# A mixture-of-experts block: single-pass products for the slot table, two gathers moved into the router's stage, the output bias moved behind the first turned rows

## What is computed

```python
logits = xt @ w_router + b_router                      # 512 tokens, 32 experts
top_v, top_e = lax.top_k(logits, 4)
weights = jax.nn.softmax(top_v, axis=-1)
# each expert e, on the rows of its tokens:
hcat = x_pad[tok] @ w1[e] + b1[e]                      # 1024 -> 2048
act = x_glu * sigmoid(1.702 * x_glu) * (x_lin + 1.0)
y = act @ w2[e] + b2[e]                                # 1024 -> 1024
out = sum over the 4 chosen experts of y * weight
x = x + g_f * out
```

## Time and profile before

| | us |
|---|---|
| median of 3 runs | 3260.22 |
| lowest and highest of them | 3252.39, 3261.88 |
| the profiled execution | 3259.38 |
| its span | 3257.5 |
| TensorE busy in the span | 3024.5 (93%) |
| VectorE busy | 2098.2 (64%) |
| ScalarE busy | 1633.2 (50%) |
| GpSimd busy | 229.2 (7%) |
| DMA, mean over the span | 187 GB/s |

### The profile page before, as it was taken

One profiled execution on the slowest core, in us unless ns is written; L12 is line 12 of the kernel. 1 busy time (PEld: TensorE's weight loads), 2 busy tenths in 40 slices (PEclk: granted clock), 3 DMA queues, 4 the chain that ended last, 5 costly groups with the idle time before them and its releaser, 6 DMA issues. The chain is left out here.

```text
span 3257.5 us, 46689 instructions
## 1 busy us (share of the span) xinstructions
PE 3024.5 (93%) x18822; PEld 2410.6 (74%) x18822; DVE 2098.2 (64%) x2112; ACT 1633.2 (50%) x1797; POOL 229.2 (7%) x141
## 2 busy tenths in 40 slices
PE   7999999879999999999999829788999999989999
PEld 2677788658877888778878717687778887778877
DVE  6536643558899999999999845466363345356633
ACT  7445532337777777777777624222453343333321
POOL 0000000001111111111111000342000000000000
PEclk9899999869999999999999969898998898999999
DMA  8321122249999999999999752000221112323322
GB/s 359 112 64 59 53 91 91 106 194 355 382 371 365 372 378 378 370 369 373 380 367 376 285 196 65 15 4 3 88 64 56 59 54 78 104 77 102 93 78 77
DMA packets 212528, 607.97 MB, mean 187 GB/s; under 512 B 9522, under 2 KB 117042, under 8 KB 176020
## 3 DMA queue, kind: packets, MB, share of 16 engines
q1 hardware_dynamic: 203008, 571.66, 47.9%
q0 software_dynamic: 9216, 33.56, 2.7%
q10 hardware_dynamic: 148, 0.53, 0.0%
HBM read 582.62 MB, written 23.10 MB: 186 GB/s over the span
## 5 line engine op out<-in xcount | busy, mean ns | idle before, releaser
L2436 DVE TENSOR_TENSOR weight_ring_part<-weight_ring,weight_ring_part 128x2048 fp32r<-128x2048 f32 x380 | 851.4, 2289 | 106.1 <-ACT weight_ring_part L2374 106.1
L2374 ACT ACTIVATE weight_ring_part<-weight_ring 128x2048 fp32r<-128x2048 f32 x380 | 711.9, 1914 | 254.6 <-DMA weight_ring<-in_w 134.0
L193 PE MATMUL ps<-weight_ring_part 128*128 128x512 f32 x1456 | 583.2, 401 | 0.0
L293 DVE TENSOR_TENSOR weight_ring_part<-weight_ring,weight_ring_part 128x2048 fp32r<-128x2048 f32 x135 | 307.5, 2283 | 292.4 <-ACT weight_ring_part L290 290.0
L189 PE MATMUL ps<-weight_ring_part,gathered_hi 128*128 128x512 f32 x1024 | 403.9, 394 | 0.0
L192 PE MATMUL ps<-weight_ring_part,gathered_lo 128*128 128x512 f32 x1024 | 400.3, 391 | 0.0
L193 PE MATMUL ps<-weight_ring_part,gathered_hi 128*128 128x512 f32 x1024 | 400.1, 391 | 0.0
L189 PE MATMUL ps<-h1T_hi,weight_ring_part 128*128 128x512 f32 x872 | 361.4, 414 | 3.2 <-DVE weight_ring_part L293 1.7
L192 PE MATMUL ps<-h1T_hi,weight_ring_part 128*128 128x512 f32 x872 | 351.5, 403 | 0.0
L290 ACT ACTIVATE weight_ring_part<-weight_ring 128x2048 fp32r<-128x2048 f32 x135 | 256.6, 1903 | 160.8 <-PE ps L193 108.3
L193 PEld LDWEIGHTS ps<-weight_ring_part 128*128 128x128 f32 x1456 | 279.3, 192 | 68.9
(11 more groups left out here) (474 smaller groups left out, 4412.5 us busy)
## 6 DMA issues: line engine op xcount, KB each, us to landing
weight_ring<-in_w SPq DMA_DIRECT2D x190, 2048.0 KB, 9.7
weight_ring<-in_w_in SPq DMA_DIRECT2D x58, 1024.0 KB, 5.3
weight_ring<-in_w_ada SPq DMA_DIRECT2D x24, 1024.0 KB, 15.0
weight_ring<-in_w_ffn_up SPq DMA_DIRECT2D x44, 512.0 KB, 4.7
weight_ring<-in_w_ffn_down SPq DMA_DIRECT2D x11, 1024.0 KB, 4.9
weight_ring<-in_w_branch SPq DMA_DIRECT2D x6, 1024.0 KB, 5.1
x_tok<-in_x SPq DMA_DIRECT2D x2, 2048.0 KB, 14.0
weight_ring<-in_w_out SPq DMA_DIRECT2D x4, 1024.0 KB, 5.2
```

Source lines behind the costliest of these rows:

```text
L193: return nc.tensor.matmul(out, x[0], y[1], start=False, stop=stop)
L293: self.nc.vector.tensor_tensor(lo, full, hi, ALU.subtract).then_inc(self.split, 1)
L2374: nc.scalar.activation(hi_half(h), full_half(h), ACT.Copy).then_inc(w_rounded, 1)
L2436: nc.vector.tensor_tensor(lo_half(h), full_half(h), hi_half(h), ALU.subtract).then_inc(w_split, 1)
```

## The change

Three edits.

1. `slot_hot` and `hot_row` become rounded fp32 tiles, so that each product of the slot table is one pass. Its numbers have to be small whole numbers for that: the choice is coded as j + 1 instead of j - 2048, and `read_tables` puts the rest back with a prepared column `spare_row`. A new drain behind the reading of `x_at` gives GpSimd leave.
2. `x_rows` and the semaphores `gathered` are made ahead of the router's stage, and GpSimd issues the gathers of experts 0 and 1 in it, as soon as `x_at` is read and the rows are stored. In the experts' stage it begins with the gather of expert 2.
3. All four bias products use banks 6 and 7 and each waits for the addition of the one before. The first stands behind `turn_inputs(0)`; the second behind the first up product; the third behind `turn_inputs` of expert 1; the fourth behind the turned hidden rows of the first turn. VectorE adds the first behind the split of the first rows, the second where the last was, the third between the hidden rows and the split of the second rows, the fourth at the end of the first turn.

```diff
-        hot_row = sb(moe, "hot_row", [P, TOPK, TT, 2, E])
+        hot_row = sb(moe, "hot_row", [P, TOPK, TT, 2, E], F32R)
+        x_rows = sb(moe, "gathered_rows", [P, 2, D])
+        gathered = [ctx.enter_context(nc.semaphore(f"gathered{n}")) for n in range(2)]
...
-        spare = sb(moe, "spare_row", [P, E])
+        spare = sb(moe, "spare", [P, E])
+        spare_row = sb(moe, "spare_row", [P, 1])
...
-        slot_hot = sb(moe, "slot_hot", [P, TOPK * TT, P])
+        slot_hot = sb(moe, "slot_hot", [P, TOPK * TT, P], F32R)
...
-        def read_tables(nc, dve):
+        def read_tables(nc, dve, read):
 
             nc.vector.tensor_copy(x_at[:, :], ps[:, 5, 0:E])
-            nc.vector.tensor_scalar(spare[:, :], ps[:, 5, E:2 * E], 0.0, col("token"), ALU.is_ge, ALU.mult)
+            dve.drain().then_inc(read, 1)
+            nc.vector.tensor_scalar(spare[:, :], ps[:, 5, E:2 * E], 0.0, spare_row[:, :], ALU.is_equal, ALU.mult)
             dve.drain()
-            nc.vector.scalar_tensor_tensor(spare[:, :], ps[:, 5, E:2 * E], float(TOPK * T), spare[:, :], ALU.add, ALU.add)
+            nc.vector.scalar_tensor_tensor(spare[:, :], ps[:, 5, E:2 * E], -1.0, spare[:, :], ALU.add, ALU.add)
...
+            @block.gpsimd
+            def _(pool):
+                pool.wait_ge(x_at_ready, 1)
+                pool.wait_ge(h_stored, 16 * TT)
+                for e in range(2):
+                    nc.gpsimd.indirect_dma_start(x_rows[:, e, :], None, h_rows, bass.IndirectOffsetOnAxis(x_at[:, e:e + 1], 0))\
+                        .then_inc(gathered[e], 16)
...
-                    nc.scalar.activation(hot_row[:, j, :, 1, :], hot[:, j], ACT.Copy, scale=float(j - TOPK * T)).then_inc(rows_made, 1)
+                    nc.scalar.activation(hot_row[:, j, :, 1, :], hot[:, j], ACT.Copy, scale=float(j + 1)).then_inc(rows_made, 1)
...
+                nc.vector.tensor_scalar(spare_row[:, :], col("token"), float(TOPK * T + 1), None, ALU.add)
...
-                read_tables(nc, dve)
+                read_tables(nc, dve, x_at_ready)
...
-                b2_banks = lambda t: ps[:, (0, 2, 6, 6)[t]:(0, 2, 6, 6)[t] + 2, :]
+                b2_banks = ps[:, 6:8, :]
...
-                        for e in range(3):
+                        for e in range(0 if rounds else 2, 3):
                             gather(r, e)
...
                     def output_bias(t_):
-                        if t_ == 3:
-                            pe.wait_ge(b2_added, 3)
+                        if t_:
+                            pe.wait_ge(b2_added, t_)
...
-                        else:
-                            output_bias(0)
-                            output_bias(1)
                         if rounds:
                             pe.wait_ge(table_read, t.block)
                         turn_inputs(0, t.nth)
                         if not rounds:
-                            output_bias(2)
+                            output_bias(0)
 
                     def turn(t):
                         if not t.last:
                             up(t)
                         if t.first and not rounds:
-                            output_bias(3)
+                            output_bias(1)
                         if not t.first:
                             pe.wait_ge(hid_ready, t.i * 2)
                         if t.more:
                             turn_inputs(1 - t.parity, t.nth_after)
+                            if t.first and not rounds:
+                                output_bias(2)
...
                                 last.then_inc(turned, 1)
+                            if t.first and not rounds:
+                                output_bias(3)
...
                         if not rounds:
-                            add_bias(0)
-                            add_bias(1)
-                            dve.drain().then_inc(up_read, 1)
+                            nc.vector.engine_nop().then_inc(up_read, 1)
...
                         split_inputs(t.i + 1)
                         if not rounds:
-                            add_bias(2)
+                            add_bias(0)
...
                             if t.first and not rounds:
-                                add_bias(3)
+                                add_bias(1)
                             split_half(t, 11)
...
                                     .then_inc(hidden_ready, 1)
+                            if t.first and not rounds:
+                                add_bias(2)
                             if t.more:
                                 split_inputs(t.i + 2)
                             if not t.first:
                                 for o in range(12, 16):
                                     split_half(t, o)
+                            if t.first and not rounds:
+                                add_bias(3)
```

More of the change, by code:

```diff
@@ L1936, in build @@
                    "logits_ready", "hot_made", "rows_made", "tops_ready", "exps_ready", "chosen_ready", "places_ready", "slots_ready", "table_ready",
-                   "weights_ready", "weights_turned") as (
+                   "weights_ready", "weights_turned", "x_at_ready") as (
                 block, *norm_sems, tables_loaded, first_rounded, hf_even, hf_odd, h_turned, h_ready, h_stored, turned_logits, logits_copied,
                 logits_ready, hot_made, rows_made, tops_ready, exps_ready, chosen_ready, places_ready, slots_ready, table_ready,
-                weights_ready, weights_turned):
+                weights_ready, weights_turned, x_at_ready):
             norm_turned = norm_sems[3]
@@ L2109, in build @@
         experts = ctx.enter_context(ExitStack())
-        x_rows = sb(experts, "gathered_rows", [P, 2, D])
         xg_hi = sb(experts, "gathered_hi", [P, DK, P], F32R)
@@ L2121, in build @@
         LIMIT = 7.0
-        gathered = [ctx.enter_context(nc.semaphore(f"gathered{n}")) for n in range(2)]
         y_stored = [ctx.enter_context(nc.semaphore(f"y_stored{n}")) for n in range(2)]
@@ L2194, in experts_pass @@
                        "glu_ready", "act_ready", "hidden_ready", "turned", "hid_rounded", "hid_ready", "y_read", "y_free",
-                       "b1_loaded", "b1_rounded", "b1_ready", "w_rounded", "w_split", "b2_summed", "b2_added") as (
+                       "b1_loaded", "b1_rounded", "b1_ready", "w_rounded", "w_split", "b2_summed", "b2_added", "x_at_ready") as (
                     block, hot_ready, table_ready, table_read, x_turned, xg_rounded, xg_ready, up_read,
                     glu_ready, act_ready, hidden_ready, turned, hid_rounded, hid_ready, y_read, y_free,
-                    b1_loaded, b1_rounded, b1_ready, w_rounded, w_split, b2_summed, b2_added):
-                b2_banks = lambda t: ps[:, (0, 2, 6, 6)[t]:(0, 2, 6, 6)[t] + 2, :]
+                    b1_loaded, b1_rounded, b1_ready, w_rounded, w_split, b2_summed, b2_added, x_at_ready):
+                b2_banks = ps[:, 6:8, :]
                 b1 = a["b1"][0]
@@ L2319, in output_bias @@
                     def output_bias(t_):
-                        if t_ == 3:
-                            pe.wait_ge(b2_added, 3)
+                        if t_:
+                            pe.wait_ge(b2_added, t_)
                         for j in range(2):
-                            last = nc.tensor.matmul(b2_banks(t_)[:, j, :], weight_et[:, P * t_:P * t_ + P],
+                            last = nc.tensor.matmul(b2_banks[:, j, :], weight_et[:, P * t_:P * t_ + P],
                                                     bias_rows2[:, 512 * j:512 * j + 512], start=True, stop=True)
@@ L2450, in add_bias @@
                         dve.wait_ge(b2_summed, t_ + 1)
-                        nc.vector.tensor_tensor(x_tok[:, t_, :], x_tok[:, t_, :], b2_banks(t_).rearrange("p b n -> p (b n)"), ALU.add)\
+                        nc.vector.tensor_tensor(x_tok[:, t_, :], x_tok[:, t_, :], b2_banks.rearrange("p b n -> p (b n)"), ALU.add)\
                             .then_inc(b2_added, 1)
```

## The result

| | before | after |
|---|---|---|
| median, us | 3260.22 (5 runs, 3252.39 to 3262.32) | 3273.8 (5 runs, 3266.4 to 3277.73) |
| ratio | | 1.0042, 95% 1.0023 to 1.0061 |
| profiled execution, us | 3259.38 (span 3257.5) | 3266.4 (span 3264.5), the fastest of its five |

The change made the kernel slower by 13.6 us (7.5 to 19.9 by the interval); 8.6 us faster was forecast. The time lies outside the stated range of 3244 to 3260 us.

A forecast was written before the change was run, and what follows sets the result against it. The prediction took the expert loop as bound by nearly always busy TensorE, with the weight stream almost as full, so an earlier start shortens everything. Terms -13.8 + 5.2 = -8.6 us gave 3251 us, range 3244 to 3260.

The forecast's parts named there:

- So the loop has a fixed length, and it ends earlier by as much as its first product starts earlier: Expert loop: TensorE nearly always busy, weight stream almost full, so an earlier first product shortens the whole time equally.
- idle time growing beyond 9.3 us: Expert loop, 733 to 1850 us: TensorE's wait for split weights growing past 9.3 us would show the prediction wrong.
- Table, 3.6 us; stage 3.4 us earlier: Router's tail: 16 table records instead of 32, read 3.6 us earlier; less 0.17 us for a drain, stage ends 3.4 earlier.
- Rounded type on VectorE, 0 to 0.8 us: One-hot tiles of the slot table: rounded output costs nothing, or 0.8 us for 16 tiles if the fast form is lost.
- It issues two gathers by about 661.7, where it had nothing to do, so the barrier is not held: GpSimd in the router's stage: both early gathers issued by about 661.7 us, with no delay to the stage's end.
- the 3.2 us of its other estimate: First early gather: estimate drawn from the Trainium skill's DMA page, 3.2 us for its 512 KB.
- First up product 7.7 us into the stage: Expert stage start: turning 2.0 us, one bias product 3.7, b1 preload 2.0, then the up product at 673.8 us.
- Gain 13.8 us: Up to the first up product: 3.4 us from the table, 10.4 from the gather wait and products ahead of it.
- Loss 5.2 us in the first turn: Moved bias products there cost 1.5 and 3.7 us; second up product 44.6 us behind the first, not 39.4.
- The two together, 8.6 us: Whole kernel: gain of 13.8 us less loss of 5.2 us makes it 8.6 us faster.
- The clock comes back sooner: Rival, expert stage start and first turn: unbroken thin products raise TensorE's clock earlier; 3243.8 us, in part 3246; chance 0.16.
- The clock stays down: Rival, first two up products: thin products ahead keep TensorE at half clock; 3290 us, or 3270 for half; chance 0.05.

The follow-up runs named there:

- The 32 bytes alone: The kernel before with an unused column of 32 bytes ahead of the split tiles of gathered rows, nothing else: 3275.33 us against 3262.01, ratio 1.0036.
- c_full: The kernel after with one early gather instead of two, split rows and split hidden rows both at 128 modulo 256: 3251.38 us against 3265.72 before, ratio 0.9953.
- the kernel with the distance restored: The kernel after with 224 unused bytes ahead of gathered_hi: 3255.75 us, ratio 0.9986 against the kernel before.

## Why the prediction was wrong

The step that failed is in its first part: "So the loop has a fixed length, and it ends earlier by as much as its first product starts earlier." The loop's length hung on a thing that the prediction never costed: the start of the tiles in SBUF. The up products' term is 96 products by 32 experts by 0.0064 us, 19.7 us. Waits for split weights, which stood among the down products, gave most of it back. What is left in the profiled executions is 0.6 us between the first and the second up product and 6.6 in the rest of the loop (1160.0 against 1153.4 us), 7.2 in all. Loops at the fast pitch scatter between 1149.6 and 1153.4 us, so against the shortest of them it is 11. The 32 bytes alone measured 13.3 us on whole runs, with an interval from 6.5 to 17.3.

The closing part named idle time growing beyond 9.3 us as a sign of error. It shrank: a loop that gets longer with less idle time has slower instructions.

The other points:
- *Table, 3.6 us; stage 3.4 us earlier*: right. From the first product of the table to VectorE's reading of it are 3.63 us instead of 7.10, so 3.5. From the table's start to ScalarE's last copy it is 9.42 us, 3.26 less than before's 12.68.
- *Rounded type on VectorE, 0 to 0.8 us*: 0, the 16 tiles take 3.23 us as in the earlier trace rows. What the prediction took from the Trainium skill ("VectorE: DVE Perf Modes", "What auto-detection actually checks"), that the fast form asks for one source and both ends in SBUF and for no type (and for even or equal sizes, which stand here), agrees with this: the trace now has the row with a rounded output that was missing.
- *"It issues two gathers by about 661.7, where it had nothing to do, so the barrier is not held"*: wrong, a mis-sized term. The issue took no time from the stage, but the barrier waits for the landing: +1.6 us. The prediction set the landing against the first use of the rows (T), where it was free, and not against the barrier, which it must meet about 1.3 us earlier. It also put the landing at 664.3, from the lower end of 4.8 us; the gathers took 5.1 and 5.3 us, the second issued 1.4 us behind the first. The 3.2 us of its other estimate were further off still.
- *First up product 7.7 us into the stage*: right, 676.44 less 668.86 is 7.6.
- *Gain 13.8 us*: 12.15 measured, less by the barrier.
- *Loss 5.2 us in the first turn*: right. After: 45.95 from up to up instead of 44.6, of which 0.6 is the slower pitch and about 0.8 a clock that came back 5.3 instead of 3.6 us behind the first dense product. With a fast pitch and 3.6 us (c_full): 44.6.
- *The two together, 8.6 us*: right where nothing else comes in. In c_full, with one early gather and aligned tiles, it is 18.31 us from the table to the first up product and 44.61 to the second, against 32.02 and 39.40: 8.5 us less.
- *The clock comes back sooner*: didn't happen. This row is the first of the kernel after whose length shows it rise, 5.3 us behind the first up product:

```profile
681.73 0.47 PE L189 MATMUL ps<-weight_ring_part,gathered_hi 128*128 128x512 f32 x1
```

- *The clock stays down*, the rival on the slow side: didn't happen either. The page's granted clock of the kernel after, answering to the earlier trace rows, has a shallower dip in the ninth slice (0.7, not 0.6) and nothing new in the loop:

```profile
PEclk9899999979999999999999969799998888999999
```

So the slow side was reached by a mechanism that no rival held. Up to the end of the expert loop the traces close: -8.6 as forecast, + 1.6 barrier, + 0.8 clock, + 7.2 slower products, in sum + 1.0 us. Measured it is the same: -12.15 up to the first up product, + 6.55 to the second, + 6.6 to the last down product. The profiled execution is 7.0 us above its counterpart; 1.0 of the other 6.0 stood there before the table began, and 5.0 came in behind the expert loop, in stages whose instructions the change leaves alone. The traces can't say what made these 5.0: kernels with the same instructions there took from 1369 to 1384 us for that part. The five runs of the kernel after give 13.6, with an interval from 7.5 to 19.9. So 6.5 us of it at least are accounted for by no row, or 2.7 if the shortest of the fast loops stands for before (+ 1.0 + 3.8). The fall from there to the kernel with the distance restored is clear of noise (ratios 1.0042 and 0.9986, intervals apart), so placement is most of the miss; how much of it arises outside the loop stays open.
